# Three routed feed-forward tails: last down weights split into used buffers, products and scatter by halves, tile 1 added later, output by tiles

## The reference, cut to what matters

```python
y = 0                                      # _hier_moe; _moe_swiglu is alike
for e in range(MOE_EXPERTS):
    hid = silu(t @ w_gate[e]) * (t @ w_up[e])
    y = y + gate[:, e:e + 1] * (hid @ w_down[e])
x = _layer_norm(DEEPNORM_ALPHA * x + ffn, ln2_g[i], ln2_b[i])   # after _hier_moe
h = h + _moe_swiglu(hn, ...)                                    # the last step: the output
```

## Time and profile before

| what | value |
|---|---|
| median of 3 runs | 2142.24 us (2141.05 to 2142.54) |
| span of the profiled execution | 2140.5 us |
| PE busy | 2077.1 us (97%) |
| PE weight load busy | 1700.6 us (79%) |
| DVE busy | 1700.4 us (79%) |
| ACT busy | 1418.6 us (66%) |
| chain that ended last | PE 84%, DVE 9%, ACT 3%, DMA 2% |
| DMA | 601.60 MB, 281 GB/s over the span |

### The profile page before, as it was taken

The page is one execution under the profiler, slowest core; times in us unless marked ns, Lnnn a source line. Parts: engine busy times, 40 slices in busy tenths (PEclk is TensorE's granted clock), DMA queues, the critical chain, the costliest instruction groups (busy, mean ns, idle before and its releaser), DMA issues.

```text
span 2140.5 us, 30902 instructions
## 1 busy us (share of the span) xinstructions
PE 2077.1 (97%) x10092; PEld 1700.6 (79%) x10092; DVE 1700.4 (79%) x2276; ACT 1418.6 (66%) x1889; POOL 130.8 (6%) x122
## 2 busy tenths in 40 slices
PE   8999999999998999999899999999999999999998
PEld 7876787867887887887776888888888888888887
DVE  4755998747997657445776999999999999999996
ACT  5662885444884634444442888888888888888885
POOL 1000100001000001111110100000000000000000
PEclk9999999999999999999999999999999999999999
DMA  7317895426993455551342899999999999999995
GB/s 275 136 74 288 345 411 197 170 91 236 412 393 107 184 219 212 200 199 74 136 177 99 319 380 384 374 381 386 368 390 378 381 377 389 370 385 380 365 404 198
DMA packets 88343, 601.60 MB, mean 281 GB/s; under 512 B 10336, under 2 KB 10400, under 8 KB 19776
## 3 DMA queue, kind: packets, MB, share of 16 engines
q1 hardware_dynamic: 79744, 570.40, 67.4%
q0 software_dynamic: 8512, 30.05, 4.6%
HBM read 585.11 MB, written 15.30 MB: 281 GB/s over the span
## 4 chain that ended last, share of the span: by engine, by line
PE 84%; DVE 9%; ACT 3%; DMA 2%; issue 2%; POOL 0%; DVEq 0%; SPq 0%; ACTq 0%; POOLq 0%
PE bank L512 24%; PE bank L514 24%; PE bank L513 24%; PE bank L1055 2%; PE bank L1515 2%; PE bank L639 1%; DVE gu_lo L1877 1%; DMA ffw_gu<-in_gate_up_m 1%; PE bank L2995 1%; DVE pj_lo L549 1%; PE bank L453 1%; DVE small L393 1%; DVE dn_lo L1877 1%; PE bank L1557 1%; DMA pieces<-in_pieces 1%
## 5 line engine op out<-in xcount | busy, mean ns | idle before, releaser
L1877 DVE TENSOR_TENSOR gu_lo<-ffw_gu,gu_hi 128x1024 fp32r<-128x1024 f32 x620 | 754.4, 1235 | 93.1 <-ACT gu_hi L1692 79.0
L1692 ACT CAST gu_hi<-ffw_gu 128x1024 fp32r<-128x1024 f32 x620 | 649.2, 1052 | 84.8 <-PE bank L514 45.3
L512 PE MATMUL bank<-gu_hi,xg_lo 128*128 128x512 f32 x1152 | 461.3, 400 | 0.0
L514 PE MATMUL bank<-gu_hi,xg_hi 128*128 128x512 f32 x1152 | 450.5, 391 | 0.0
L513 PE MATMUL bank<-gu_lo,xg_hi 128*128 128x512 f32 x1152 | 449.6, 390 | 0.0
L1877 DVE TENSOR_TENSOR dn_lo<-ffw_d,dn_hi 128x1024 fp32r<-128x1024 f32 x299 | 365.2, 1229 | 26.5 <-ACT dn_hi L1700 17.1
L1700 ACT CAST dn_hi<-ffw_d 128x1024 fp32r<-128x1024 f32 x310 | 326.5, 1056 | 63.1 <-PE bank L514 56.0
L512 PE MATMUL bank<-dn_hi,hidt_lo 128*128 128x512 f32 x664 | 260.1, 392 | 6.3 <-DVE hidt_lo L1877 6.1
L514 PE MATMUL bank<-dn_hi,hidt_hi 128*128 128x512 f32 x664 | 258.5, 389 | 0.0
L513 PE MATMUL bank<-dn_lo,hidt_hi 128*128 128x512 f32 x664 | 258.4, 389 | 0.0
L514 PEld LDWEIGHTS bank<-gu_hi,xg_hi 128*128 128x128 f32 x1152 | 216.2, 188 | 45.8
(11 more groups left out here) (444 smaller groups left out, 2692.2 us busy)
## 6 DMA issues: line engine op xcount, KB each, us to landing
ffw_gu<-in_gate_up_m SPq DMA_DIRECT2D x288, 1024.0 KB, 7.1
ffw_d<-in_down_m SPq DMA_DIRECT2D x144, 1024.0 KB, 9.0
pieces<-in_pieces SPq DMA_DIRECT2D x70, 1024.0 KB, 6.9
ffw_gu<-in_gate_up_ff SPq DMA_DIRECT2D x22, 1024.0 KB, 6.8
ffw_d<-in_down_ff SPq DMA_DIRECT2D x11, 1024.0 KB, 8.7
h<-token_sums POOLq DMA_DIRECT2D x3, 1024.0 KB, 7.4
pieces<-in_pieces SPq DMA_DIRECT2D x4, 512.0 KB, 8.0
norm_vec<-in_ln_g POOLq DMA_DIRECT2D x4, 512.0 KB, 4.5
```

The source lines that it names most:

```text
L512: nc.tensor.matmul(bank, a_lo, b_hi, start=start, stop=False)
L514: return nc.tensor.matmul(bank, a_hi, b_hi, start=False, stop=stop)
L1692: nc.scalar.copy(gu_hi[:, 2 * k:2 * k + 2, :], ffw_gu[:, blk["slot"], 2 * k:2 * k + 2, :])\
L1877: return V.tensor_tensor(out, x, hi.bitcast(F32), ALU.subtract)
```

## The change

Five things change in the tails of m0, m1 and m2.

1. The last step's down weights are split into the parts of `gu_hi` and `gu_lo` that held pieces 0 and 1 of the same step's gate and up weights. ACT makes both copies before the last silu and waits only until TensorE has used that piece. DVE takes the lo parts around the last hidden product. In m0 and m1 the quarters of the next mixer's piece 0 move behind: ACT does quarter 0 first, 1 after the silu, 2 and 3 after the last `hidt_hi`; DVE does quarter 3 between the two halves of `yg_lo`.
2. The last down products run half by half (columns 0 to 511 for both f, then 512 to 1023), with a semaphore after the first half. The filling matmuls before and after them go.
3. Sums and scatter run by halves: rounding, `yg_lo`, and four scatter matmuls for half 0 of both tiles; then `keep_busy_tensor(0, 3)` and the four for half 1.
4. DVE adds tile 0 only. In m0 and m1 it normalizes tile 0, then adds tile 1 (`second_sums_vector`), then goes on: in m0 `x_lo` of tile 0 comes ahead of tile 1's statistics, in m1 tile 0's features, tile 1's statistics, `x_lo` of tile 0.
5. In m2 the output is stored as two transfers of 512 KB, each after its tile's additions. The overflow flag is read on DVE ahead of the units; the overflow code gets the additions of tile 1 and a few more matmuls, which run only when the flag is set.

```diff
+    SCATTER_BANK = ((5, 6), (2, 7))
...
+    def last_down_parts(f):
+        return (gu_hi[:, 2 * f:2 * f + 2, :].rearrange("p c n -> p (c n)"),
+                gu_lo[:, 2 * f:2 * f + 2, :].rearrange("p c n -> p (c n)"))
+
+    def last_down_tensor(pe, st):
+        pe.wait_ge(sem("hidt_split"), st["s"] + 1)
+        for half in range(2):
+            cols = slice(half * 512, (half + 1) * 512)
+            for f in range(2):
+                if half == 0:
+                    pe.wait_ge(sem(f"down_split{f}"), st["G"] + 1 + DOWN_CREDIT)
+                hi, lo = last_down_parts(f)
+                last = three_products(psum[3 + half],
+                                      (hidT_hi[:, st["par"], f, :], hidT_lo[:, st["par"], f, :]),
+                                      (hi[:, cols], lo[:, cols]), False, f == 1)
+            if half == 0:
+                last.then_inc(sem("first_sums"), 1)
+            else:
+                last.then_inc(sem("down_piece"), DOWN_PIECES)
...
-    def scatter_tensor(pe, t, j, banks):
-        pe.wait_ge(sem("yg_split"), ROUTER[t] + 1)
-        for half in range(2):
+    def scatter_tensor(pe, t, half):
+        pe.wait_ge(sem("yg_split"), 2 * ROUTER[t] + half + 1)
+        for j in range(T):
             for part, src in enumerate((yg_lo, yg_hi)):
-                last = nc.tensor.matmul(psum[banks[half]], pick_r[:, j, :], src[:, half * 512:(half + 1) * 512],
-                                        start=(part == 0), stop=(part == 1))
+                last = nc.tensor.matmul(psum[SCATTER_BANK[j][half]], pick_r[:, j, :],
+                                        src[:, half * 512:(half + 1) * 512], start=(part == 0), stop=(part == 1))
             last.then_inc(sem("scattered"), 1)
...
-                keep_busy_tensor(0, 5)
-                down_tensor(pe, last, True)
-                keep_busy_tensor(0, 9)
-                scatter_tensor(pe, t, 0, (5, 6))
-                scatter_tensor(pe, t, 1, (2, 7))
+                last_down_tensor(pe, last)
+                scatter_tensor(pe, t, 0)
+                keep_busy_tensor(0, 3)
+                scatter_tensor(pe, t, 1)
...
+    def last_down_hi_scalar(act, st, f):
+
+        if f == 0:
+            act.wait_ge(sem(f"down_landed{st['slot']}"), 16 * st["uses"])
+        act.wait_ge(sem("gu_piece"), GU_PIECES * st["s"] + f + 1 + GU_USED)
+        nc.scalar.copy(last_down_parts(f)[0], ffw_d[:, st["slot"], f, :]).then_inc(sem("down_hi_ready"), 1)
...
-        act.wait_ge(sem("down_piece"), DOWN_PIECES * (last["s"] + 1) + DOWN_USED)
         for half in range(2):
+            if half == 0:
+                act.wait_ge(sem("first_sums"), ROUTER[t] + 1)
+            else:
+                act.wait_ge(sem("down_piece"), DOWN_PIECES * (last["s"] + 1) + DOWN_USED)
             nc.scalar.copy(yg_hi[:, half * 512:(half + 1) * 512], psum[3 + half]).then_inc(sem("yg_hi_ready"), 1)
...
+            def last_step(st, prev):
+                next_piece_scalar(act, t, (0,))
+                hidt_hi_scalar(act, prev)
+                for f in range(2):
+                    last_down_hi_scalar(act, st, f)
+                silu_scalar(act, st)
+                next_piece_scalar(act, t, (1,))
+                hidt_hi_scalar(act, st)
+                next_piece_scalar(act, t, (2,))
+                pickr_scalar(act, t)
+                next_piece_scalar(act, t, (3,))
...
+    def last_down_lo_vector(dve, st, f):
+
+        dve.wait_ge(sem("down_hi_ready"), DOWN_PIECES * st["G"] + f + 1)
+        hi, lo = last_down_parts(f)
+        rest(lo, ffw_d[:, st["slot"], f, :], hi).then_inc(sem(f"down_split{f}"), 1)
...
-    def sums_add_vector(dve, t, j, banks):
+    def sums_add_vector(dve, t, j, read):
 
         dve.wait_ge(sem("scratch_moved"), 16 * SUMS_MOVED[t])
         for half in range(2):
-            dve.wait_ge(sem("scattered"), 4 * ROUTER[t] + 2 * j + half + 1)
+            dve.wait_ge(sem("scattered"), 4 * ROUTER[t] + 2 * half + j + 1)
             hv = h[:, j, half * 512:(half + 1) * 512]
-            V.tensor_tensor(hv, psum[banks[half]], hv, ALU.add).then_inc(sem("scatter_read"), 1)
+            V.tensor_tensor(hv, psum[SCATTER_BANK[j][half]], hv, ALU.add).then_inc(read, 1)
+
+    def second_sums_vector(dve, t):
+
+        sums_add_vector(dve, t, 1, sem("scatter_read"))
+        dve.wait_ge(sem("scatter_read"), 4 * (ROUTER[t] + 1))
...
-    def sums_lo_vector(dve, t):
-        for half in range(2):
-            dve.wait_ge(sem("yg_hi_ready"), 2 * ROUTER[t] + half + 1)
-            cols = slice(half * 512, (half + 1) * 512)
-            last = rest(yg_lo[:, cols], psum[3 + half], yg_hi[:, cols])
-        last.then_inc(sem("yg_split"), 1)
+    def sums_lo_vector(dve, t, half):
+        dve.wait_ge(sem("yg_hi_ready"), 2 * ROUTER[t] + half + 1)
+        cols = slice(half * 512, (half + 1) * 512)
+        rest(yg_lo[:, cols], psum[3 + half], yg_hi[:, cols]).then_inc(sem("yg_split"), 1)
...
+            def last_step(st, prev):
+                next_piece_vector(dve, t, (0,))
+                hidt_lo_vector(dve, prev)
+                last_down_lo_vector(dve, st, 0)
+                hidden_vector(dve, st)
+                last_down_lo_vector(dve, st, 1)
+                hidt_lo_vector(dve, st)
+                next_piece_vector(dve, t, (1, 2))
...
-                sums_lo_vector(dve, t)
-                sums_add_vector(dve, t, 0, (5, 6))
-                sums_add_vector(dve, t, 1, (2, 7))
+                sums_lo_vector(dve, t, 0)
+                next_piece_vector(dve, t, (3,))
+                sums_lo_vector(dve, t, 1)
+                sums_add_vector(dve, t, 0, sem("scatter_read"))
...
+        flag = overflow_flag(dve, t)
         units(dve, t, unit)
-        flag = overflow_flag(dve, t)
-        dve.wait_ge(sem("scatter_read"), 4 * (ROUTER[t] + 1))
+        dve.wait_ge(sem("scatter_read"), 4 * ROUTER[t] + 2)
         overflow_vector(dve, t, flag)
...
+            for bank in SCATTER_BANK[1]:
+                for c in range(4):
+                    last = nc.tensor.matmul(psum[bank][:, c * P:(c + 1) * P], ident, mask_causal[:, 1, :], start=True, stop=True)
+            last.then_inc(done, 1)
...
+            sums_add_vector(dve, t, 1, done)
+            dve.wait_ge(done, OV_SUMS)
...
-        layer_norm_ask(1)
+        second_sums_vector(dve, t)
         if t == "m1":
             features_tile_vector("sg", 0, par["l0_mix_norm_2"], sem("xt_chunks"))
-        x_lo_tile_vector(NEXT[t], 0)
+            layer_norm_ask(1)
+            x_lo_tile_vector("sg", 0)
+        else:
+            x_lo_tile_vector("od", 0)
+            layer_norm_ask(1)
         layer_norm_center(1)
...
+        second_sums_vector(dve, "m2")
+        dve.sem_inc(sem("phase_done"), 1)
...
-            sp.wait_ge(sem("phase_done"), 8)
-            sp.dma_start(out[0].rearrange("(j p) d -> p j d", p=P), h).then_inc(sem("out_written"), 16)
-            sp.wait_ge(sem("out_written"), 16)
+            for j in range(T):
+                sp.wait_ge(sem("phase_done"), 8 + j)
+                sp.dma_start(out[0, TILES[j]], h[:, j, :]).then_inc(sem("out_written"), 16)
+            sp.wait_ge(sem("out_written"), 16 * T)
```

More of the change, by code:

```diff
@@ L1816, in unit @@
             q = q0 + u
-            def step(st, prev, following):
-                nxt = following if following is not None else (None if final else make_step(t, u + 1, 0, 0))
-                if nxt is not None:
-                    gu_hi_scalar(act, nxt, (0,))
-                else:
-                    next_piece_scalar(act, t, (0,))
+            def last_step(st, prev):
[9 more added lines that the diff above has]
+                next_piece_scalar(act, t, (3,))
+            def step(st, prev, following):
+                if following is None and final:
+                    last_step(st, prev)
+                    return
+                nxt = following if following is not None else make_step(t, u + 1, 0, 0)
+                gu_hi_scalar(act, nxt, (0,))
                 hidt_hi_scalar(act, prev)
-                if nxt is None:
-                    next_piece_scalar(act, t, (1, 2))
-                elif following is None:
+                if following is None:
                     gu_hi_scalar(act, nxt, (1,))
@@ L1833, in step @@
                 silu_scalar(act, st)
-                if nxt is not None:
-                    gu_hi_scalar(act, nxt, (3,))
-                else:
-                    next_piece_scalar(act, t, (3,))
+                gu_hi_scalar(act, nxt, (3,))
                 down_hi_scalar(act, st, 0)
-                if nxt is None:
-                    hidt_hi_scalar(act, st)
                 down_hi_scalar(act, st, 1)
-                if nxt is None:
-                    pickr_scalar(act, t)
             last = middle(act, t, u, step)
@@ L1986, in unit @@
                 pick_vector(dve, t, u)
-            def step(st, prev, following):
```

(25 more changed lines are left out.)

3 lines of the change are left out of this document (2 added, 1 removed).

## The result

The changed kernel takes 2143.66 us (median of 20 runs, 2141.26 to 2149.87), the kernel before 2141.05 us (20 runs, 2138.72 to 2144.52). The ratio is 1.0014, 95% interval [1.0008, 1.0020]: **2.6 us slower** where 7.2 us less were forecast. The profiled execution took 2148.0 us, with a span of 2146.1, so it is one of the longer ones. One execution of experiment 10 took 3495.84 us at a granted clock of 0.557 and is left out of its figures.

A forecast was written before the change was run, and what follows sets the result against it. TensorE bounds most of the span (84% of the chain), but the tails were taken as a serial relay. Gains of 2.0 (m0), 2.0 (m1) and 3.2 (m2), 7.2 us, from 2142.24 gave 2135.0 us; range 2133.0 to 2138.5.

The forecast's parts named there:

- Parts 1 to 4: Routed tails: last down products start 1.34 us earlier, sums and scatter run by halves; m0 and m1 gain 2.0 us each.
- The thin margins: Last step of the tails: moved weight copies end 0.3 us before the silu; cover for the products 0.3 to 0.4 us.
- Part 4: m0 and m1: tile 0 normalized 3.45 us earlier, tile 1's h 2.05 us earlier; each gains 2.0 us.
- Part 5: End of m2: second store issued 1.9 us earlier and landing 1.3 us sooner; 3.2 us gained.
- The second store: End of m2: half the output lands in 3.4 us instead of 4.7, worth 1.3 us.
- the forecast's 78.3: Sum of the three tails from the last silu: 26.4 in m0, 36.8 in m1, 15.0 in m2.
- the five: Rivals: m0 clock falls (0.22, 0.08), store no faster (0.10), products no earlier (0.08), m1 low clock shorter (0.03), slower (0.04).
- The clock in m0: Gap of 2.8 us before tile 1's transposes lowers TensorE's clock: 1.7 us lost (chance 0.22) or 3.4 (0.08).
- The slower rival: Clock stays low through projections behind m0's and m1's gaps; 19 us more low clock would give 2144.5 us; chance 0.04.

The follow-up runs named there:

- experiment 10: Kernel before with 22 filling matmuls added at TensorE's start; 2141.72 us, ratio to before 1.0001.
- experiment 1: Changed kernel with the piece load of m0 and m1 issued only after tile 1 is normalized; 2138.15 us, ratio to before 0.9982.
- experiment 8: experiment 5 plus filling passes: 10 ahead of tile 1's transposes in m0, 17 ahead of m1's first products; 2132.74 us, ratio 0.9959.
- experiment 7: Changed kernel with the late piece load and 22 filling matmuls added at TensorE's start; 2133.86 us (one run).
- experiment 5: Changed kernel with the late piece load and the 22 filling passes put ahead of the flag read and branch; 2133.07 us, ratio 0.9965.
- experiment 9: Changed kernel, piece load unmoved, with 22 filling matmuls added at TensorE's start; 2138.0 us, ratio to before 0.9989.
- Experiment 11: experiment 5 plus 22 filling matmuls at TensorE's start; 2134.09 us, ratio to before 0.9965.
- experiment 6: Changed kernel, piece load unmoved, with the 22 filling passes put ahead of the flag read and branch; 2134.78 us, ratio 0.9967.

## Why the prediction was wrong

**Parts 1 to 4 were right where nothing else stood in the way.** In m2, from the silu: scatter at 6.00 us (forecast 2128.30 - 2122.30 = 6.0), second scatter at 7.63 (forecast 7.8), second store issued at 11.2 (forecast 11.2). The thin margins held: the silu wasn't delayed. In m0 the statistics of tile 0 start 9.33 us behind the silu, before 13.04; that is 3.7 us where 3.45 was put down. Part 4 shows where no gap disturbs it: m1 gained 2.8 us in experiment 1 and m0 2.4 us in experiment 8, with its clock held, where 2.0 was forecast for each.

**Part 5 was right, its sum 0.5 us short.** 3.74 us measured, 3.2 forecast. With one store it is 2.56: 1.84 from the earlier issue and 0.7 since that store landed in 4.0 us and not in the 4.7 of the earlier trace rows; the kernels with the old tail gave 4.7, 5.0 and 5.2. The second store brings 1.18 where 1.3 was put. The Trainium skill's rule of at least 1 MiB in a transfer (DMA: Bandwidth & Descriptors, Rules for kernel authors) is for the most bandwidth. Read as a price for the last store, as the prediction read it, it would have made the term nothing, and the trace disagrees (1.18 us).

**The step that failed is two sentences on what is around the tail.** The first: "The next mixer's piece 0 is split about 4.7 us later in m0 and m1, and the load of the piece after next with it. That one is read some 35 us later, so it costs nothing". It was right that the load is read late, but the load was priced by its reader only. It also has neighbours: for 6 us it keeps the 16 DMA engines 81% busy, and it was moved from a stretch in which TensorE ran 28 fillings and products into the one in which TensorE jumps. The second: "The overflow code is skipped." To skip it is a taken branch, and the code behind it must be there. Before, that wait didn't show: the trace has 0.32 us of it in m1 and none in m0, where the packet started at 356.44, ahead of the scatter (356.81). The old tail could also have borne some of it, since its 44 fillings ended 1.1 us before tile 0's transposes; the change took that slack to nothing (in experiment 7 the transposes follow the last filling at once), and no part of the forecast counts it. Moving the load back gains 6.7 us in the tails (89.38 to 82.65), and putting the fillings ahead of the branch 4.4 more (82.65 to 78.30). Together that is 11.1 us. That it ends on the forecast's 78.3 is luck, as said: m0 still holds 1.66 us of low clock and m1 1.1 us of wait, and parts 4 and 5 gained more than was put down.

The Trainium skill has the rule (Runtime: NRT & Kernel Launch, Instruction fetch mechanics): code comes in blocks of 16 KiB by a DMA queue of the engine's own, and a taken branch to a place that isn't loaded makes the engine wait for it. The trace agrees in kind: the instruction packets of that queue are 16,384 bytes, one comes through in each gap, and the gaps move with the place of the code. The Trainium skill gives no price for such a branch; here the gap, with the fillings behind the branch, was up to 3.2 us with a quiet DMA and 1.9 to 5.9 us beside a load.

**The rivals.** None of the five was this one. The clock in m0 came as priced (1.66 us, forecast 1.7) and was taken for possible at 0.30; it shows in experiments 5, 7, 9 and 11, whose m0 tails are 27.7 to 27.8 us, and not in experiment 6, with the same idle time of 2.72 us and a tail of 26.70. The slower rival (0.04) had the wrong mechanism: not 14 us of low clock, but idle time ahead of work in program order. In m0 the gap takes 5.89 us, and the low clock on the 44 fillings behind it adds only 6.87 - 5.18 = 1.7.

**Open.** That the gap is a code fetch is inferred from four things (the "issue" label, the effect of place and load, the start of the instruction packets, and the 1.2 to 1.5 us from a packet's end to TensorE's next work), not from a record that names it. Whether the order of fillings and branch works by covering the wait or by a luckier place of the code is settled in part. Experiment 11 can't tell for m0, since experiments 7 and 9, with the same shift and the fillings behind the branch, have no gap there either. Experiments 5 and 6 say more: their TensorE code is the same, and in m0 the packet starts 8.57 us behind the silu without a load and 12.12 us with it. In 6 it ends at 13.09, and the transposes start at 14.55, 1.46 behind it and 0.51 later than in 5, though VectorE had tile 0 ready at 13.9 in both. So that wait ran beside the fillings and the normalization, and all but 0.5 us of it was covered. What isn't shown is how much of m0's gain in experiment 5 the order brings and how much the place. In m1 the wait stayed in all four kernels with the fillings first. What decides whether the clock falls behind an idle stretch of 2.7 us is open too.

## What to carry to other kernels

Price a moved DMA twice: for the one who reads it, and for whoever needs the DMA engines at the moment to which it is moved, the engines' own code among them. Dummy or otherwise unneeded work that stands in program order between a branch and the next needed instruction adds to the wait for code; put it ahead of the branch, where it can run beside that wait. When an edit has left its own steps as forecast and the time is off all the same, look for "issue" gaps behind branches, and shift the code by some instructions as a control before believing a difference of a few microseconds.

## What the runs showed of the hardware that was not expected

A branch over code that isn't executed cost TensorE nothing in one layout, 1.92 and 3.19 us in others with the DMA engines at 2%, and 5.29 and 5.89 us with a load of 2 MB in flight at 322 GB/s. The packet of code takes about 1 us in both cases and starts 2.8 to 3.5 us later beside the load, so the fetch queues with the data. The wait need not stand at the branch itself: it came behind 7 fillings in experiment 9 and behind 29 in m1 of the changed kernel. The same 22 matmuls at the very start of TensorE's code moved the gap from m0 to m1, some 350 us into the kernel and 650. Behind an idle stretch of 2.67 us in m0 the granted clock was 0.50 in the changed kernel, behind one of 2.72 it was 0.68 over the next 3 us in experiment 5 and 1.00 in experiment 6. A store of 512 KB at the end landed in 2.8 to 3.3 us (the median of the two in each run), one of 1 MB in 4.0 to 5.2.
